# Two last stages of a float32 network kernel: one weight tile times both parts of the activation as a single 512-column matmul

## The reference, cut to what matters

```python
def sq_relu_mlp(h, w1, w2):
    return jnp.square(jax.nn.relu(h @ w1)) @ w2
...
        hl = modulate(rms_norm(xl, norm2_g[i]), mod_l[3], mod_l[4])
        xl = xl + mod_l[5][:, None, :] * sq_relu_mlp(hl, w_ff1[i], w_ff2[i])
```

## Time and profile before

| | us |
|---|---|
| median of 3 runs | 1525.32 (1522.89 to 1527.55) |
| the profiled execution | 1528.37 |
| its span, first to last instruction | 1526.6 |
| TensorE busy in the span | 1440.9 |
| VectorE, ScalarE, GpSimd busy | 912.7, 590.0, 413.6 |
| ff1b, first to last matmul of the stage | 1331.6 to 1430.7 |
| ff2b | 1430.7 to 1523.1 |

### The profile page before, as it was taken

One profiled execution on the slowest core, in us unless ns is written; L12 is line 12 of the kernel. 1 busy time (PEld: TensorE's weight loads), 2 busy tenths in 40 slices (PEclk: granted clock), 3 DMA queues, 4 the chain that ended last, 5 costly groups with the idle time before them and its releaser, 6 DMA issues.

```text
span 1526.6 us, 24609 instructions
## 1 busy us (share of the span) xinstructions
PE 1440.9 (94%) x10592; PEld 1246.3 (82%) x10592; DVE 912.7 (60%) x1091; ACT 590.0 (39%) x719; POOL 413.6 (27%) x322
## 2 busy tenths in 40 slices
PE   5789989989999998999899999999999998899999
PEld 5678989989999996764477888888886955799999
DVE  7966545466778667867638777255425478534343
ACT  5524364444334454210623322323224356334433
POOL 4998712100003400000002343443320010034553
PEclk9899999999999999999899999999999999999999
DMA  8333333565767565875426654344423500545552
GB/s 270 118 110 111 113 109 135 177 202 166 228 231 237 178 219 176 240 225 130 160 86 217 195 177 154 124 152 138 137 83 111 176 18 9 187 141 189 183 178 82
DMA packets 158259, 239.37 MB, mean 157 GB/s; under 512 B 5680, under 2 KB 128592, under 8 KB 158032
## 3 DMA queue, kind: packets, MB, share of 16 engines
q1 hardware_dynamic: 153360, 232.85, 46.4%
q10 hardware_dynamic: 4800, 5.08, 1.3%
HBM read 227.55 MB, written 1.05 MB: 150 GB/s over the span
## 4 chain that ended last, share of the span: by engine, by line
PE 83%; DVE 6%; POOL 5%; ACT 4%; issue 2%; DMA 1%; DVEq 0%; SPq 0%; ACTq 0%; POOLq 0%
PE bank L2054 24%; PE bank L2055 24%; PE bank L2056 23%; PE bank L2362 2%; PE bank L2118 1%; PE bank L2530 1%; POOL A L1937 1%; POOL A L1910 1%; POOL X L1908 1%; ACT whi L661 1%; PE bank L2519 1%; DVE wlo L1120 1%; DVE stat L1795 1%; PE bank L2241 1%; DMA A<-in_w_mod 1%
## 5 line engine op out<-in xcount | busy, mean ns | idle before, releaser
L2054 PE MATMUL bank<-ahi,whi 128*128 128x256 f32 (+1 forms) x2480 | 793.2, 320 | 24.5 <-POOL alo L605 7.8
L2055 PE MATMUL bank<-alo,whi 128*128 128x256 f32 (+1 forms) x2480 | 784.0, 316 | 0.0
L2056 PE MATMUL bank<-ahi,wlo 128*128 128x256 f32 (+1 forms) x2480 | 783.4, 316 | 0.0
L1120 DVE TENSOR_TENSOR wlo<-raw,whi 128x2048 fp32r<-128x2048 f32 x160 | 366.7, 2292 | 387.3 <-ACT whi L661 387.0
L661 ACT ACTIVATE whi<-raw 128x2048 fp32r<-128x2048 f32 x160 | 306.3, 1914 | 731.6 <-PE bank L2056 731.6
L2054 PEld LDWEIGHTS bank<-ahi,whi 128*128 128x128 f32 x2480 | 478.2, 193 | 72.3 <-issue 28.0
L2056 PEld LDWEIGHTS bank<-ahi,wlo 128*128 128x128 f32 x2480 | 478.1, 193 | 28.8
L2055 PEld LDWEIGHTS bank<-alo,whi 128*128 128x128 f32 x2480 | 478.3, 193 | 26.8 <-issue 0.2
L2021 POOL TENSOR_TENSOR A<-A 128x512 f32 (+1 forms) x48 | 106.8, 2237 | 490.4 <-ACT A L986 490.4
L2003 POOL TENSOR_TENSOR alo<-A,ahi 128x512 fp32r<-128x512 f32 (+1 forms) x43 | 126.5, 2944 | 354.5 <-ACT ahi L860 354.5
L1477 DVE SCALAR_TENSOR_TENSOR A<-modraw,scc,A 128x1024 f32<-128x1024 f32 x60 | 105.0, 1789 | 0.6
(11 more groups left out here) (305 smaller groups left out, 1227.1 us busy)
## 6 DMA issues: line engine op xcount, KB each, us to landing
raw<-in_w_ff SPq DMA_DIRECT2D x64, 1024.0 KB, 5.2
modraw<-in_w_mod SPq DMA_DIRECT2D x72, 512.0 KB, 4.6
raw<-in_w_in SPq DMA_DIRECT2D x28, 1024.0 KB, 5.1
A<-in_w_mod SPq DMA_DIRECT2D x24, 512.0 KB, 5.1
raw<-in_pw SPq DMA_DIRECT2D x12, 1024.0 KB, 7.3
raw<-in_w_ffn_gate SPq DMA_DIRECT2D x11, 1024.0 KB, 5.3
raw<-in_w_ffn_up SPq DMA_DIRECT2D x11, 1024.0 KB, 5.4
raw<-in_w_ffn_down SPq DMA_DIRECT2D x11, 1024.0 KB, 5.1
```

Of the source, the lines that this page charges most:

```text
L1120: dve.tensor_tensor(wlo[:, k % 2, :], raw[:, (k + 2) % 4, :], whi[:, k % 2, :].bitcast(F32), ALU.subtract).then_inc(wlo_ready, 1)
L2054: pe.matmul(out_, w_hi, a_hi, start=start, stop=False, **kw)
L2055: pe.matmul(out_, w_hi, a_lo, start=False, stop=False, **kw)
L2056: return pe.matmul(out_, w_lo, a_hi, start=False, stop=stop, **kw)
```

## The change

Three things, in ff1b and ff2b alone:

1. ahi and alo become the two halves of one tensor `apair`. `joined` issues whi x [ahi | alo] as one matmul of 512 columns, which fills a whole bank: whi x ahi in its columns 0 to 255, whi x alo in 256 to 511. A second matmul adds wlo x ahi to columns 0 to 255. So two matmuls take the place of three, and the two halves of the bank have yet to be added.
2. ff1b: a block fills two banks (0 and 1, or 2 and 3) in place of half as much. ScalarE copies the two upper halves to `rl`, VectorE adds the lower ones and makes max(x, 0) times x in one instruction into `hid`. Relu and GpSimd's squares are gone. TensorE waits before block p for the hidden features of block p-2 (`hid_sq`).
3. ff2b: eight chunks in eight banks, 0 to 7, in place of four. TensorE waits for the hidden features of block 15 before its first block. At the end each chunk is added to X in two steps, upper half and lower half, the second waiting for the first.

```diff
-        ahi = sb("ahi", [P, 4096], F32R)
-        alo = sb("alo", [P, 4096], F32R)
+        apair = sb("apair", [P, 2, 4096], F32R)
+        ahi, alo = apair[:, 0, :], apair[:, 1, :]
...
-                one = ph[0] == "ff1b"
-                for m in range(1 if one else 2):
...
+                if ph[0] == "ff1b":
+                    if p.least >= 2:
+                        act.wait_ge(hid_sq, 32 + p.l - 1)
+                    for m in range(2):
+                        i = act.activation(rl[:, p.least % 2, T1 * m:T1 * m + T1],
+                                           pb[2 * (p.k % 2) + m][:, T1:2 * T1], ACT.Copy)
+                    i.then_inc(half_out, 1)
+                    return
...
             def dve_ff1b(p):
                 ahead(p)
+                dve.wait_ge(half_out, p.l + 1)
+                for m in range(2):
+                    half = rl[:, p.least % 2, T1 * m:T1 * m + T1]
+                    i = dve.tensor_tensor(half, pb[2 * (p.k % 2) + m][:, 0:T1], half, ALU.add)
+                link(i)
+                dve.scalar_tensor_tensor(hid[:, bass.ds(512 * p.l, 512)], rl[:, p.least % 2, :], 0.0, rl[:, p.least % 2, :],
+                                         ALU.max, ALU.mult).then_inc(hid_sq, 1)
...
             for c in range(8):
-                if c % 2 == 0:
-                    wait_bank("ff2b", c // 2, 4)
-                gated_add(1, 5, c, 0, pb[4 + c // 2][:, 256 * (c % 2):256 * (c % 2) + 256]).then_inc(evac["ff2b"], 1)
+                wait_bank("ff2b", c, 8)
+                link(gated_add(1, 5, c, 0, pb[c][:, T1:2 * T1]))
+                gated_add(1, 5, c, 0, pb[c][:, 0:T1]).then_inc(evac["ff2b"], 1)
...
-            squares_of(32, 0, 14)
             hidden_lo(27, 0, 2, 512, hid, 2048)
-            squares_of(32, 14, 16)
             hidden_lo(27, 2, 16, 512, hid, 2048)
...
+            def joined(bank, w_hi, w_lo, x0, start, stop):
+
+                pe.matmul(bank[:, :].rearrange("p (a t) -> p a t", a=2), w_hi, apair[:, :, x0:x0 + T1],
+                          start=start, stop=False, skip_group_check=True)
+                return pe.matmul(bank[:, 0:T1], w_lo, ahi[:, x0:x0 + T1], start=False, stop=stop, skip_group_check=True)
+
+            def joined_feature_block(p, chunk_wait):
+
+                pe.wait_ge(wlo_ready, p.b + 1)
+                (wh, wl), w = tiles(p, KD)
+                for m in range(2):
+                    for c in range(KD):
+                        if chunk_wait and m == 0:
+                            chunk_wait(c)
+                        mm = joined(pb[2 * (p.k % 2) + m], wh[:, c, P * m:P * m + P], wl[:, c, P * m:P * m + P],
+                                    T1 * c, c == 0, c == KD - 1)
+                mm.then_inc(block_done, 1)
+
+            def joined_row_block(p, at, last):
+
+                pe.wait_ge(wlo_ready, p.b + 1)
+                (wh, wl), _ = tiles(p, 2)
+                s = at + 2 * T1 * (p.least % 4)
+                for c, m in ([(c, m) for m in range(8) for c in range(2)] if last else
+                             [(c, m) for c in range(2) for m in range(8)]):
+                    mm = joined(pb[m], wh[:, c, P * m:P * m + P], wl[:, c, P * m:P * m + P], s + T1 * c,
+                                p.least == 0 and c == 0, last and c == 1)
+                    if last and c == 1 and m < 7:
+                        mm.then_inc(bank_done, 1)
+                mm.then_inc(block_done, 1)
...
             def pe_ff1b(p):
                 if p.least == 1:
                     mod_turn(11)
-                pe_ff1(p, True, 6)
+                if p.least >= 2:
+                    pe.wait_ge(hid_sq, 32 + p.l - 1)
+                joined_feature_block(p, (lambda c: wait_norm(pe, 6, c)) if p.least == 0 else None)
...
+            def pe_ff2b(p):
+                pe.wait_ge(hlo_ready, 28 + p.l)
+                if p.least == 0:
+                    pe.wait_ge(hid_sq, 48)
+                joined_row_block(p, 2048, p.least == 15)
```

More of the change, by code:

```diff
@@ L336, in program @@
         hid_sq = sem("hidden_ready")
+        half_out = sem("upper_half_of_bank_out")
         gq_sq = sem("gq_squares")
@@ L973, in relus @@
                 act.wait_ge(block_done, p.b + 1)
-                one = ph[0] == "ff1b"
-                for m in range(1 if one else 2):
[L976 to L986, removed]
+                if ph[0] == "ff1b":
[7 more added lines that the diff above has]
+                for m in range(2):
+                    if p.least >= 1:
+                        act.wait_ge(hid_sq, p.l * 2 + m - 1)
+                    act.activation(rl[:, m, :], pb[2 * p.k + m][:, :], ACT.Relu).then_inc(relu_ready, 1)
             squares(act, 4, lambda u: [(evac["pw2"], u + 1)])
@@ L1853, in dve_ff1b @@
                 ahead(p)
+                dve.wait_ge(half_out, p.l + 1)
[5 more added lines that the diff above has]
+                                         ALU.max, ALU.mult).then_inc(hid_sq, 1)
                 if p.least == 2:
                     store_mods(1, 12, 5, 1, 6)
-            each_block(dve, "ff1b", dve_ff1b)
+            each_block(dve, "ff1b", dve_ff1b, roll=False)
             ph[0] = "ff2b"
@@ L2578, in pe_ff1b @@
                     mod_turn(11)
-                pe_ff1(p, True, 6)
+                if p.least >= 2:
+                    pe.wait_ge(hid_sq, 32 + p.l - 1)
+                joined_feature_block(p, (lambda c: wait_norm(pe, 6, c)) if p.least == 0 else None)
             each_block(pe, "ff1b", pe_ff1b)
             pe.wait_ge(mod_ready, 9)
-            each_block(pe, "ff2b", lambda p: pe_ff2(p, "ff2b", 27, 2048, 256))
+            def pe_ff2b(p):
[3 more added lines that the diff above has]
+                joined_row_block(p, 2048, p.least == 15)
+            each_block(pe, "ff2b", pe_ff2b)
 def chunked(v, n=KD):
```

## The result

| | before | after |
|---|---|---|
| median of 20 runs each, side by side, us | 1526.91 | 1534.07 |
| ratio after / before | | 1.0054, interval 1.0044 to 1.0063 |
| the profiled execution, us | 1528.37 | 1532.87 |
| its span | 1526.6 | 1531.1 |

The ratio is +8.2 us, between 6.7 and 9.6, where +7.0 was forecast. A later repeat gave 1.0051 (1.0031 to 1.0070), which is +7.8. The change makes the kernel slower, by the wait at the change of stage above all.

What follows compares the result with a forecast made beforehand. TensorE's stream was taken as the bound, busy 94% of the span. Gain -6.7, stalls +4.0, turn's wait +0.1, stage change +6.1, clock +1.8 and tail +1.7 sum to +7.0: 1532.3 us, range 1528 to 1539.

Steps and rivals of the forecast that it cites:

- Gain: Joined tiles in ff1b and ff2b take 346.7 ns for 360, 0.213 us less a block: -6.7 us in all.
- Rival 1: A joined matmul pays for both halves, so a tile stays at 360 ns: +12.5 us, 1537.8; chance 0.12.
- rival 2: The 13.3 ns is the weight load, partly hidden, so a tile takes 320 ns: -2.5 us, 1522.8; chance 0.05.
- The chain in ff1b: TensorE waits for VectorE's sums behind wlo, 0.57 us at seven odd blocks, 3 to 15: +4.0 us.
- the prediction's own sign of being wrong: Wrong if the stage-change wait is much under 6 us, or ff1b blocks alternate other than 5.55 and 6.12.
- Blocks 0 and 1: First ff1b blocks, at low clock: some 0.3 us saved together, 0.1 longer wait for the modulation row.
- Change of stage: ff2b, now in all eight banks, waits uncovered for the sum of ff1b's last block: +6.1 us.
- Clock: After the wait of six us, the granted clock falls at the start of ff2b: +1.8 us (1.4 to 2.3).
- Tail: Sixteen linked sums at the end, 0.92 us a bank, finish 2.6 us after TensorE: +1.7 us (1.3 to 2.5).
- GpSimd: Without ff1b's squares GpSimd is 41 us less busy, worth nothing since TensorE did not wait for it.
- rival 3: Chain shorter than counted, clock stays up over the stage change: +3.1 us, 1528.4; chance 0.12.
- rival 4: The clock falls in ff1b's stalls too, seven pairs losing some 10 us: +17 us, 1542; chance 0.03.

Runs made afterwards that it cites:

- e3: Changed kernel with ff1b's copies, adds and max-and-multiply ahead of the weight conversions; ratio 1.0003 to the kernel before.
- e4: e3 plus banks 4 to 7 first in ff2b's block 0, the wait for ff1b's last sum behind them; ratio 0.9967, again 0.9974, to the kernel before.
- e4b: Changed kernel with only banks 4 to 7 first in ff2b's block 0, sums not moved ahead; ratio 1.0033 to the kernel before.
- e2: Only ff2b joined, ff1b as before the change with Relu and GpSimd squares; ratio 1.0014 to the kernel before.
- e7: e4 with one extra TensorE wait at block 3 of ff2b (three intended, one made); one run, 1525.52 us.
- e5: e4 with ff2b's upper halves added early, during blocks 14 and 15, leaving eight sums at the end; ratio 0.9970, again 0.9963, to the kernel before.
- b6: Kernel before with block 0 of ff1b emptying its bank and copying the modulation row ahead of the weight conversion; ratio 0.9966 to the kernel before.
- e6: e5 with the modulation row copied ahead of the weight conversion in block 0 of ff1b; ratio 0.9945 to the kernel before.

## Why the prediction was right

- **Gain.** The mechanism was right, the pitch was not the only one. 226.7 + 120.0 = 346.7 ns was seen in four of eleven profiles in ff2b; after had 353.3. So the term -6.7 is mis-sized: ff2b gave 15 x 0.107 = 1.6 us from its tiles where 3.2 were forecast. Rival 1 (360) and rival 2 (320) are out.
- **The rule of the Trainium skill.** A joined tile saves 13.3 or 6.7 ns against three matmuls. The Trainium skill, "TensorE: Matmul & The Clock Gate", section "Wait — 56ns, not 53.3ns?", has about 2.5 ns for a dropped back-to-back matmul and says nothing there of a weight load ahead of each, as all have here; this case's trace doesn't agree with 2.5 in either pitch.
- **The chain in ff1b.** The mechanism was right: wlo at n + 2.2, adds, max-and-multiply 0.69 for the 0.743 taken, end at n + 5.9, and waits for L1859 within ff1b at the seven odd blocks from 3 on and no others. e3 shows the cause: with the sums ahead the stalls are gone. The sizes were off both ways. The odd blocks start 0.3 to 0.4 us late and their first tile takes 0.1 more, 0.4 to 0.5 for the 0.57: seven are 3.0 us for the 4.0. The other 1.0 us in blocks 2 to 15 comes from five blocks at 353.3 ns (0.5) and from first tiles up to 0.1 longer in some even blocks (0.4). So +1.0 for the +1.0 forecast is in part luck, and the prediction's own sign of being wrong was met as it is worded: blocks alternate 5.65 to 5.76 and 5.95 to 6.02, not 5.55 and 6.12, and the idle times are 0.14 to 0.24, not 0.5 to 0.6. The pair hardly depends on the pitch, since the chain sets where its second block starts: 11.61 and 11.62 us for 11.67.
- **Blocks 0 and 1.** -0.2 for -0.2 is luck too: the second profile of after has -1.1.
- **Change of stage.** 6.13 us later than its slot, for 6.1. e3, e4 and e4b take it away in pieces.
- **Clock.** The fall was right, 1.8 us was too little: block 0 of ff2b took 8.11 us, 2.5 over its 5.65 (1.8 in the second profile; 2.3 was the high bound). The rows it was taken from lie elsewhere: block 1 had 7.12 us at 0.78 after a wait of 2.82, but waits of 2.1 to 3.0 us within a full stream (e2, e3, e4b, e7) cost no clock at all. So a wait's length alone does not give the price. A low clock ahead of the wait is not what tells them apart either: in after, block 0 of ff1b had 1.00, and block 1 behind 2.88 us fell to 0.66 all the same. TensorE had been half idle ahead of block 0, and in the other four the stream was full; whether that is the reason was not tested.
- **Tail.** +1.6 for +1.7; 0.92 us a bank, end 2.5 us after TensorE for 2.6. e5 takes it away.
- **GpSimd.** The squares' groups fell by 39.5 us, the whole engine by 35.9, for the 41 forecast; TensorE waited for them neither before nor after.
- **Rivals 3 and 4.** The chain was not much shorter (0.69, not 0.43) and the clock did fall at the change of stage, so rival 3 is out. The pairs of ff1b have a granted clock of 1.00, so rival 4 is out.
- **Sum.** Two mis-sized terms, the gain by 1.6 in ff2b and the clock by 0.7, account for the 2.3 between +9.2 and +7.0 in the profile. The second profile has +7.9, the medians +8.2 and +7.8.
- **Slips in the working.** With the max-and-multiply at its low bound of 0.43 the stalls are 7 x 0.26 = 1.8 us and not 2.2, so rival 3 adds up to +2.7. And 1.7 + 0.213 is 1.9, where 1.8 went into the sum. Neither moves the forecast by more than 0.1 us.

## What to carry to other kernels

Price a fused instruction (one that takes the place of two) by what stands behind its result: here 7 to 13 ns a tile were bought with eight banks instead of four, and with a sum that hung behind a 2.3 us conversion. At a change of stage look which buffers the next stage could start on without the last result, and order it so; that, together with the sum put ahead of the conversion, turned +8.2 into -4 to -5 us. And look for the neighbour's wait on the same critical stretch: one small copy put ahead of a conversion gave 3 to 5 us, about as much as the whole repaired fusion.

## What the runs showed of the hardware

- Streams of equal width had one pitch (120.0 and 226.7 ns). Alternating 512 and 256 columns, each with its own weight load, had two, 346.7 and 353.3 ns, steady over ff2b and different between executions of one kernel; in ff1b of after both stood in one stage.
- The granted clock stayed 1.00, the 2.4 GHz level, behind single waits of 2.1, 2.5, 2.75 and 3.0 us in an otherwise full stream, and fell behind 6.0 us, to a mean of 0.67 and 0.74 over the next block. In block 1 of ff1b it fell behind waits of 2.82 and 2.88, in after from a block 0 at 1.00 to a mean of 0.66, and stayed at 1.00 when the wait was 0.96 (b6) and 1.02 (e6).
